# The output projection's first weight slab moved ahead of the last slab of the second modulation

## The reference, cut to what matters

```python
mod1 = silu(cond) @ ada_w[1] + ada_b[1]      # the second layer's modulation, 1024 x 6144
ml   = mlstm_bidir(...)                      # 4 heads, 4 chunks of 128 tokens, two directions
ml   = rms_norm(ml) * head_norm * sigmoid(o)
cat  = concatenate([na, ml], axis=-1)        # 512 + 512 columns
out  = cat @ w_out                           # 1024 x 1024, the output projection
x    = x + gate * out                        # then the norm and the first MLP
```

## Time and profile before

| what | value |
|---|---|
| median of three runs | 2970.74 us (2968.17 to 2975.41) |
| the profiled execution's own time | 2969.91 us |
| its span, first to last instruction | 2968.1 us |
| outside the span | 1.8 us |
| PE busy | 2774.2 us, 93% |
| DVE busy, ACT busy | 57%, 39% |
| mean granted TensorE clock | 0.968 |

### The profile page before, as it was taken

How to read it: one execution, slowest core, us unless ns; L and a number is a source line. 1 busy time by engine, 2 the same in 40 slices (tenths; PEclk the granted TensorE clock), 3 DMA queues, 4 the chain that set the end, 5 groups by cost and what they waited for, 6 DMA issues and landing times. The chain is left out here.

```text
span 2968.1 us, 55702 instructions
## 1 busy us (share of the span) xinstructions
PE 2774.2 (93%) x24704; PEld 2282.0 (77%) x24704; DVE 1691.5 (57%) x2625; ACT 1147.3 (39%) x1895; POOL 198.8 (7%) x261
## 2 busy tenths in 40 slices
PE   6998878999999988989899999988999999999999
PEld 3874458989974588889498898867898997456898
DVE  3438367556551388887365554576554553575554
ACT  2235434334321445553243433534433432144432
POOL 2212210000000001000000000000000000200000
PEclk9998789999999999999999999998999999999999
DMA  9335663555532100000355555534355554414454
GB/s 289 101 114 176 230 219 114 182 187 194 178 128 85 25 8 4 4 3 4 131 196 185 170 178 182 186 109 142 114 184 182 172 179 148 159 58 142 140 173 142
DMA packets 258168, 409.31 MB, mean 138 GB/s; under 512 B 18647, under 2 KB 111208, under 8 KB 257800
## 3 DMA queue, kind: packets, MB, share of 16 engines
q1 hardware_dynamic: 253832, 392.50, 38.6%
q0 software_dynamic: 4096, 13.25, 1.8%
HBM read 400.68 MB, written 2.95 MB: 136 GB/s over the span
## 5 line engine op out<-in xcount | busy, mean ns | idle before, releaser
L352 DVE TENSOR_TENSOR ring_parts<-ring,arena_parts 128x2048 fp32r<-128x2048 f32 x270 | 598.9, 2256 | 284.4 <-ACT arena_parts L345 282.1
L345 ACT CAST arena_parts<-ring 128x2048 fp32r<-128x2048 f32 x270 | 495.4, 1885 | 517.7 <-PE psum L2895 229.3
L2895 PE MATMUL psum<-arena_parts 128*128 128x256 f32 x2816 | 512.5, 285 | 2.4 <-DVE arena_parts L580 2.1
L2895 PEld LDWEIGHTS psum<-arena_parts 128*128 128x128 f32 x2816 | 443.3, 194 | 3.7 <-DVE arena_parts L580 3.0
L2895 PE MATMUL psum<-arena_parts,ring_parts 128*128 128x256 f32 x1408 | 400.7, 285 | 0.0
L389 PE MATMUL psum<-arena_parts 128*128 128x512 f32 x1024 | 327.1, 393 | 2.0 <-DVE arena_parts L580 2.0
L2895 PEld LDWEIGHTS psum<-arena_parts,ring_parts 128*128 128x128 f32 x1408 | 272.8, 194 | 0.0
L1915 PE MATMUL psum<-arena_parts 128*128 128x512 f32 x768 | 236.7, 390 | 0.0
L389 PEld LDWEIGHTS psum<-arena_parts 128*128 128x128 f32 x1024 | 194.0, 190 | 43.2 <-DVE arena_parts L580 2.7
L389 PE MATMUL psum<-ring_parts,arena_parts 128*128 128x512 f32 x560 | 219.6, 392 | 0.0
L1897 PE MATMUL psum<-arena_parts 128*128 128x256 f32 x896 | 163.3, 285 | 4.3 <-DVE ring_parts L352 4.3
(11 more groups left out here) (505 smaller groups left out, 5188.7 us busy)
## 6 DMA issues: line engine op xcount, KB each, us to landing
ring<-in_mlp_w SPq DMA_DIRECT2D x48, 2048.0 KB, 8.3
ring<-in_ada_w SPq DMA_DIRECT2D x24, 2048.0 KB, 8.5
ring<-in_ffn_pre_w_gu SPq DMA_DIRECT2D x44, 1024.0 KB, 7.3
ring<-in_ffn_post_w_gu SPq DMA_DIRECT2D x44, 1024.0 KB, 6.7
ring<-in_ffn_pre_w_down SPq DMA_DIRECT2D x8, 2048.0 KB, 7.8
ring<-in_xmem_wkv SPq DMA_DIRECT2D x8, 2048.0 KB, 8.2
ring<-in_ffn_post_w_down SPq DMA_DIRECT2D x8, 2048.0 KB, 7.8
ring<-in_ab_w_in SPq DMA_DIRECT2D x7, 2048.0 KB, 12.5
```

The lines of the kernel that those rows point to most:

```text
L345: nc.scalar.copy(high_view(name)[:, k, :], raw_view(name)[:, k, :]).then_inc(*up(act, ("high", name, h)))
L352: nc.vector.tensor_tensor(low_view(name)[:, k, :], raw_view(name)[:, k, :], high_view(name).bitcast(F32)[:, k, :], ALU.subtract)\
L2895: ins = nc.tensor.matmul(psum[:, b, 256 * j:256 * j + 256], s[:, k, at:at + P], x_parts[q][:, k, :], start=(k == 0 and i == 0), stop=(k == ...
```

## The change

In the list of slabs the first `ab_out` slab goes ahead of the last `ada1` slab. The new numbers are 30 for `ada1` 10, 31 for `ab_out` 0, 32 for `ada1` 11 and 33 for `ab_out` 1. In `ml_pe` the last two chunks (i = 14 and 15) no longer run a filling step, so that 21 of the 24 steps are done when it ends. The last filling, which then has three steps, moves behind `ab_out_pe(0, 0)`.

```diff
         plan_ada(0, 4, 8)
-        plan_ada(1, 0, 12)
-        plan_rows("ab_out", a["ab_w_out"][0], KT, D)
+        plan_ada(1, 0, 11)
+        plan(("ab_out", 0, 0), a["ab_w_out"][0], KT, 0, 512)
+        plan_ada(1, 11, 1)
+        plan(("ab_out", 1, 0), a["ab_w_out"][0], KT, 512, 512)
...
-                        if z:
+                        if z and i < 14:
                             fill(pe, queue, 1)
...
             ml_pe(pe, ada[2])
+            ab_out_pe(pe, 0, 0)
             fill(pe, ada[2], 4)
-            ab_out_pe(pe, 0, 0)
             merge_pe(pe)
```

## The result

| | kernel before | changed kernel |
|---|---|---|
| median on this chip | 2971.68 us (8 runs, 2968.17 to 2975.41) | 2979.53 us (8 runs, 2976.16 to 2984.11) |
| ratio to before | | 1.0027, 95% interval 1.0016 to 1.0038 |
| the profiled execution: own time, span | 2969.91, 2968.1 us | 2981.3, 2979.5 us |

The changed kernel was slower, by 7.9 us in this comparison. In the file of the changed kernel every line from the edit on has moved by 2: line 1849 is the projection (1847 before), 1824 the high part, 1752 and 1741 the merge, 852 `ada_turn`, 822 the modulation, 347 the MLP's split.

The account below looks back on a forecast made before the run. It took slab fetches, landing 5.4 us apart, to bound PE's wait ahead of line 1847. An earlier start of 5.40 us against 7.8 us more up to line 850 gave +2.4, or 2973.1 us, range 2968.5 to 2979.0.

Parts of the forecast that it names:

- change 3: Second `ab_out` slab: issued at 408.48, landing at 416.5, `merge_act` waits behind its copy; line 850 net +2.4 us.
- Change 1: First `ab_out` slab, ahead in the queue, lands at 387.79; the projection starts at 394.64, a gain of 5.40 us.
- Change 2: Three filling steps on PE, moved behind `ab_out_pe(0, 0)`: +2.98 us after its unchanged 12.71 us, nearly hidden behind DVE.
- Change 4: `mlp0` slabs: issued at 439.85, landing at 448.2 to 449, wanted by ACT at 451.1; no cost.
- rival (b): Two MLP slabs issued together share the DMA engines; first lands at 453.5; +4.8 us, 2975.5 us; chance 0.15.
- (a): Second `ab_out` slab arrives before `merge_act` could start, or ACT isn't held; -4.0 us, 2966.7 us; chance 0.08.
- (c): Slab 31 lands later than 387.79; gain lost, extra 7.8 us stays, 2978.5 us; chance 0.07.

Follow-up runs that it names:

- act_order: The changed kernel with ACT's merge copies put ahead of the high part of the projection's second slab; ratio to the kernel before 0.9993.
- fetch_only: The changed kernel with PE's order of the kernel before, so that only the order of fetches differs from before; ratio to the kernel before 0.9985.
- steps_only: The kernel before with only PE's order changed, three half steps behind the projection's first half, fetches in the old order; ratio to the kernel before 1.0044.
- after_again: The changed kernel without an edit, executed and profiled once more; ratio to the kernel before 1.0012.
- step22_act: The changed kernel with the first moved half step back in the mLSTM and ACT's merge copies ahead of the second slab's high part; ratio to before 0.9980.
- late_half: The changed kernel with columns 0 to 511 of the projection's weights in the late slab instead of 512 to 1023; 2970.34 us, one execution.

## Why the prediction was wrong, step by step

I had +2.4 us and a range to 2979.0; +7.9 and 2979.53 came. The mechanism of change 3 was the one that the traces and `act_order` show. The step that failed is its sum up to line 850: the projection's 12.71 us, kept as before, were 13.80, and the fetch's 8.0 us were 9.17. With them the +2.4 at that line became +4.64. What is left of the 7.9 is mostly scatter, and the range had too little room for that.

- **Change 1, the earlier slab: right.** ACT's first copy starts 20.50 us behind A (in the changed kernel's first profile, as all numbers here); foretold were 387.79 - 367.22 = 20.57. From that copy to PE's product it is 6.85 us, to the hundredth. The gain is 5.47 for 5.40.
- **Change 2, the three steps: right in kind, 1.1 us short.** The steps cost 2.78 for 2.98 us and lie beside the fetch. But I kept the projection's 12.71 us, "because the idle time ahead of it is still over 8 us". It took 13.80: 12 of its products were slow (rows of 0.6 us and more, as those of before from 400.04 on), not 7. The windows view of the changed kernel has the clock at half in this stretch, the 1.2 GHz level:

```profile
401.00:404.00 3.00, 3.00 (x8) 2.33 (x8) 2.96 (x3) 0.00 (x0) 0.00 (x0) 0.50 0.00 0
```

  In the eight profiles in which the steps leave the gap, slow products (rows over 0.5 us) number 11 to 13; with them at its start, 7 and 8; with them right ahead of the projection (`fetch_only`), none. The length of the idle time doesn't explain it: 10.32 us ahead of the 7 and 8, 7.5 to 8.2 ahead of most of the 11 to 13, and 14.84 ahead of the 12 of `steps_only`. So the half steps in the gap, which I had costed at nothing, did pay: with them PE's next recovery was shorter. It was the term that I should have priced when I took away their place.
- **Change 3, the late fetch: right, with one term mis-sized.** Issue 1.13 us behind step 22 (1.13 foretold), landing 9.17 (8.0 taken; I had put 9.1 as the upper bound), high part and next start 1.80 (1.79), first tile 1.24 (1.2), DVE 4.23 (4.23). Together with the clock: 1.09 + 1.17 = 2.26 us over the sum, which takes +2.4 at line 850 to the +4.64 measured (58.78 - 54.14 behind A); in `after_again` it was +4.90. The Trainium skill's fit ("DMA: Bandwidth & Descriptors", section "Anatomy of one DMA — SWDGE (gpsimd) path"), which gave an estimate of 6.8 us, is the furthest from the 9.2.
- **Change 4, the MLP's slabs: right.** They went out at 449.17 and 449.6. Behind A that is 3.3 us later than foretold (75.89 for 72.63), the 2.26 from above and 1.02 from below. The DMA view of the two:

```profile
DMA to landing us min/median/max: 8.4/10.9/13.3
```

  One lands at 457.6, the other some 5.3 us behind it. The first was no slower than alone, so rival (b) is refuted, and ACT's line 347 at 460.42 waited for PE, not for a DMA.
- **Behind line 850** I had expected no more. In the first profile 1.02 us came on top up to B (10 slow products in `ab_out_pe(0, 1)`, 4 before). In `after_again` there were 2, and from the start of `ab_out_pe(0, 1)` to B it took 23.23 us against 23.68 before. So this is scatter of the clock, and not the change.
- **The rivals.** (a) would have needed a fetch under 4 us, as said, and `step22_act` shows what it is worth: line 852 4.2 us earlier than before. (c) gave 2978.5, near the median, but not by its mechanism: slab 31 landed on time. It was near by luck: 4.5 to 5.8 us of cost met 2 to 3 of scatter.
- **The range.** I had three runs, from 2968.17 to 2975.41. Of the 31 runs of the kernel before in one later comparison the lowest is 2957.61 and the highest 2977.07. A cost of 5 to 6 us puts the median at 2976 to 2977, and with the 2 to 3 us by which I took a median to be off, the upper end belonged at 2980 or above.

## What to carry to other kernels

When a step that frees a buffer is moved, follow the buffer: here 1.06 us of products sent the issue of a 2 MB fetch 23 us back (42.28 for 18.85 us behind A), and this cost time only because ACT, which works in order, had a copy of that slab queued ahead of work which was ready. Products that fill a gap may be worth more than nothing even though PE would have waited: they bear on the clock of what follows, so price both levels for the first products behind a gap that is changed. And where two executions of one kernel differ by 6 us ahead of the edit, compare between two marks around it before reading anything into the spans.

## What the runs showed of the hardware that was not expected

- The same four small products of line 1564 take 2.17 us in one execution of the kernel before and 3.78 in another, and the clock's recovery shifts the start of a stage by several us. Mark A, with the same work ahead of it, lies anywhere from 364.44 (`late_half`) to 373.28.
- A 2 MB fetch took 9.1 to 9.4 us at this place of the program in six profiles, whatever it fetched, and 7.6 to 8.4 at most others. It goes with a packet of code that is loaded meanwhile: of 154 fetches without one, none took more than 8.8 us.
